# RWKV recurrence of a hybrid decoder layer: two full 32-bit products of each turn written as sums of products of high and low halves

## The chip, the cores and the metric

The kernel runs on one core of a Trainium2 chip. The core has five engines with a queue of instructions each: TensorE (PE in the profile; its weight loads are listed apart, as PEld), VectorE (DVE), ScalarE (ACT), GpSimd (POOL) and SyncE (SP), which here only issues DMAs. Every engine works through its own queue in order and waits for others at semaphores. The metric is the device time of one execution in microseconds (us); lower is better. The median of three runs of the kernel before is 944.3 us (944.24 to 944.64).

## The reference

One layer of a decoder for 512 tokens of width 1024, in float32. A combined projection feeds an RWKV-7 branch, a short convolution and a dilated attention; their gated sum and a SwiGLU follow. The change lies in the RWKV branch:

```python
xm = p + (token_shift(p) - p) * mu
r, k, v, wl, al, gl = jnp.split(xm, RWKV_SPLITS, axis=-1)
w_log = -jax.nn.softplus(-(w0 + jnp.tanh(wl) @ w_up)) - 0.5
a = jax.nn.sigmoid(a0 + al @ a_up)
g = jax.nn.sigmoid(gl) @ g_up                       # gate: 128 -> 512 channels
...
kk = heads(k * k_k)
kk = kk * lax.rsqrt(jnp.maximum(jnp.sum(kk * kk, axis=-1, keepdims=True), 1e-12))
k = k * (1 + (a - 1) * k_a)
...
_, y = lax.scan(rwkv7_step, state0, xs)             # the recurrence
...
return (y.reshape(bsz, seq, RWKV_WIDTH) * g.astype(jnp.float32)).astype(p.dtype)
```

The two products concerned are `sigmoid(gl) @ g_up` and the sum of `kk * kk` over the 64 channels of each head.

## The kernel before

All large products are already made of halves. A float32 operand x is split into a high part, x rounded to the type fp32r by a copy, and a low part, x less the high part, by a subtraction. A product then is three fp32r matmuls: high by high, low by high and high by low. For the weights ScalarE makes `w_hi` (L876), GpSimd makes `w_lo` in four instructions (L734), and SyncE loads `w_raw` two slots ahead.

The recurrence is worked through in four turns, T = 0 to 3, of 128 tokens each (`rwkv(T)`, one function on each of TensorE, VectorE and ScalarE). The small steps of a turn depend on each other across the engines. TensorE's gaps between them are filled with the rest of the big projection, `fill(count)` and `fill_steps(count)` at L2248: matmuls of 128 rows, 128 columns of weights and 512 tokens, three for each of `KT` = 8 slices, so 24 to a tile and 12 tiles (q = 0 to 11) to a turn. The tiles alternate between the PSUM banks 6 and 7. ScalarE copies each finished tile out (L964, L967, `copy_tile`), and tile q may only start when tile q - 2 has been copied (`spill_copied`). How many filler matmuls stand between two steps is written out by hand.

In this order TensorE does, in the first part of turn T: `fill(10)` and `loras(0)` (T = 0 only; the decay's and the in-context rate's up-projections, L2263), `fill(2)` or, for T > 0, `fill(6)`, then for T = 0 only `gate(0)` (L2269) and `turn_v(0)` (transposes of v, L2275), and in each turn the sum of squares (L2286), `fill(28)` or `fill(30)` and the transposes of the recurrence's operands. For T > 0 the calls `loras(T)`, `gate(T)`, `turn_v(T)` stand near the end of the turn before; the transposes of that turn's result y (`turn_y`, L2390) come ahead of them, except at the end of turn 0, where they come behind them and three filler matmuls later.

The other engines at these places: VectorE ends a turn with the chain that normalises y, whose last instruction multiplies by the gate (L1732, `y_ready`). Then it begins the next turn with `kk` (L1585), adds the biases to the up-projections (L1590, L1592), and waits for the sum of squares (L1597). ScalarE does tanh and sigmoid of the next turn's inputs (`lora_inputs`, L986, L987) near the end of a turn, then copies tiles; in the next turn it squares kk (L992), applies a sigmoid (L994), copies the gate out of PSUM (L997, L999), loads the table for the square root (L1002), takes it, and copies tile 0. All of these stand in one queue.

`need(signal)` waits for a signal of this turn. `Signal(name, per)` counts `per` increments a turn, and `at(turn, k)` is the value after the increment k of a turn.

Of the kernel before, what the change touches and what calls it, by code (L numbers as in the profile page):

```python
# [25 lines left out]
def hybrid_layer(nc, x, norm_mix_post, norm_ffn_pre, norm_ffn_post, w_in, rwkv_w_up, rwkv_a_up, rwkv_g_up,  # L26
# [77 lines left out]
    with ExitStack() as ctx:  # L104
# [26 lines left out]
        lora_up = fixed("lora_up", [P, RW])  # L131
        g_up = fixed("g_up", [P, RW])
# [80 lines left out]
        xs, _ = arena("xs", [P, NH, HD], e)  # L213
        k2, e = arena("k2", [P, NJ, P], o)
# [3 lines left out]
        assert o <= AT_YC, (o, AT_YC)  # L218
        rk, o = arena("rk", [P, NJ, P], AT_TAIL)
        state, o = arena("state", [P, NJ, 2, HD], o)  # L220
        g_tok, o = arena("g_tok", [P, NH, HD], o)
        y1, o = arena("y1", [P, NH, HD], o)
        y2, o = arena("y2", [P, NH, HD], o)
        ln_wb, o = arena("ln_wb", [P, 2, RW], o + 4 * NJ * P)
# [85 lines left out]
        params_loaded, ups_loaded = sem("params_loaded"), sem("ups_loaded")  # L310
# [28 lines left out]
        xm_ready, lora_ready, gate_ready = Signal("xm_ready"), Signal("lora_ready"), Signal("gate_ready")  # L339
        z_done, g_done = Signal("z_done"), Signal("g_done")  # L340
        z_ready, sig_ready, sums_run, exps_ready = Signal("z_ready"), Signal("sig_ready"), Signal("sums_run"), Signal("exps_ready")
        kk_ready, sq_ready, ssq_done, ssq_ready = Signal("kk_ready"), Signal("sq_ready"), Signal("ssq_done"), Signal("ssq_ready")
# [38 lines left out]
        form_hi_ready = after_turns(gate_ready)  # L381
        form_lo_made = after_turns(z_done)
        b_hi_made = after_turns(g_done)
        b_lo_made = after_turns(z_ready)
# [3 lines left out]
        t4_made = after_turns(kk_ready)  # L388
        t12_hi_made = after_turns(sq_ready)
# [175 lines left out]
        def _(sp):  # L565
# [25 lines left out]
            sp.dma_start(lora_up[0:HD, :], rwkv_w_up[0]).then_inc(ups_loaded, 16)  # L591
            sp.dma_start(lora_up[HD:P, :], rwkv_a_up[0]).then_inc(ups_loaded, 16)
            sp.dma_start(g_up[:], rwkv_g_up[0]).then_inc(ups_loaded, 16)
# [272 lines left out]
        def _(act):  # L866
# [70 lines left out]
            for n in range(5, N_RWKV + 2):  # L937
                high(n, raw_value(n), n % 2)
# [4 lines left out]
            def rwkv(T):  # L943
# [450 lines left out]
        def _(dve):  # L1394
# [178 lines left out]
            def rwkv(T):  # L1573
# [11 lines left out]
                v.tensor_tensor(kk[:], k_, par(C_KK), ALU.mult).then_inc(kk_ready.sem, 1)  # L1585
# [8 lines left out]
                last.then_inc(z_ready.sem, 1)  # L1594
                need(ssq_done)
                need(sq_ready)
# [514 lines left out]
        def _(pe):  # L2111
# [106 lines left out]
            pe.wait_ge(ups_loaded, 48)  # L2218

            def rwkv(T):  # L2220
# [64 lines left out]
                need(sq_ready)  # L2285
                t_.matmul(ps[:, 3], head_ones[:], sq[:].rearrange("p j t -> p (j t)"), start=True, stop=True).then_inc(ssq_done.sem, 1)  # L2286
# [524 lines left out]
```

## Time and profile before

| | before |
|---|---|
| median of 3 runs | 944.3 us (944.24 to 944.64) |
| profiled execution, its own time | 944.45 us |
| its span, first to last instruction | 942.4 us |
| TensorE busy | 934.0 us, 99% of the span |
| VectorE, ScalarE, GpSimd busy | 68%, 46%, 47% |
| mean granted clock of TensorE | 0.999 of full speed |
| TensorE busy from 83.7 to 405 us (most of the recurrence) | 321.27 of 321.3 us |

The busy time of TensorE is the union of its matmuls, which overlap: a matmul of 512 columns is listed with 0.39 us and followed by the next one after 0.23 us. So what a product costs is read from where the next one starts, not from its own duration. A timeline row names start, duration, engine, line, operation, output and inputs, and in brackets how long the engine had been idle and what ended that.

### The profile page before, as it was taken

What the parts mean: (1) busy time and instruction counts of PE and PEld (TensorE: products, weight loads), DVE (VectorE), ACT (ScalarE), POOL (GpSimd) and SP (SyncE); (2) the same over time, 40 slices, a digit from 0 to 9 for tenths busy, and PEclk for the clock granted to TensorE, in tenths of its full rate; (3) what the DMA queues carried; (4) which work ended last, traced back from release to release, by engine and by line L of the source; (5) the groups of instructions that cost most, each with busy time, mean ns of one, the idle gap of its engine ahead of it and who ended that gap; (6) DMA issues with size and microseconds to landing.
All of it is one profiled execution on the core that took longest, in us unless ns stands there. A gap on an engine that the chain in (4) does not pass through costs nothing.

```text
span 942.4 us, 16115 instructions
## 1 busy us (share of the span) xinstructions
PE 934.0 (99%) x6666; PEld 787.5 (84%) x6666; DVE 639.4 (68%) x814; ACT 432.0 (46%) x626; POOL 441.5 (47%) x325
## 2 busy tenths in 40 slices
PE   9999999999999999999999999999999999999997
PEld 7888877787887778777878888888999999988886
DVE  6877967766586756899675656988989898411114
ACT  6423515723461562337753425574556555322332
POOL 4884524334263245253145653514765565555551
PEclk9999999999999999999999999999999999999999
DMA  8323332342333265229144842286566656243312
GB/s 287 116 91 114 109 113 93 117 148 70 132 108 129 81 220 182 92 80 323 68 157 151 317 144 72 78 195 161 130 149 171 154 143 174 81 145 108 114 45 89
DMA packets 110805, 128.44 MB, mean 136 GB/s; under 512 B 3216, under 2 KB 87184, under 8 KB 110736
## 3 DMA queue, kind: packets, MB, share of 16 engines
q1 hardware_dynamic: 100224, 102.64, 33.9%
q0 software_dynamic: 2880, 10.49, 5.9%
q10 hardware_dynamic: 7632, 14.32, 4.0%
q8 instruction: 52, 0.85, 0.4%
q14 instruction: 17, 0.14, 0.0%
HBM read 100.70 MB, written 16.25 MB: 124 GB/s over the span
## 4 chain that ended last, share of the span: by engine, by line
PE 53%; issue 26%; POOL 16%; DVE 4%; ACT 1%; DMA 0%; POOLq 0%; DVEq 0%; ACTq 0%
POOL w_lo L734 15%; PE ps L2116 11%; PE ps L2117 11%; PE ps L2118 11%; PE ps L2654 5%; PE ps L2656 5%; PE ps L2655 5%; PE ps L2432 2%; PE ps L2467 1%; PE ps L2484 1%; DVE bias_dil L1504 1%; DVE x_ct L1513 1%; PE ps L2458 1%; PE ps L2161 0%; DVE rstd_x L1436 0%
## 5 line engine op out<-in xcount | busy, mean ns | idle before, releaser
L734 POOL TENSOR_TENSOR w_lo<-w_raw,w_hi 128x512 fp32r<-128x512 f32 x220 | 318.5, 1477 | 378.1 <-ACT w_hi L876 377.5
L876 ACT CAST w_hi<-w_raw 128x2048 fp32r<-128x2048 f32 x55 | 105.0, 1909 | 137.9 <-PE ps L2118 106.3
L2248 PE MATMUL ps<-a_hi,w_hi 128*128 128x512 f32 x384 | 154.7, 403 | 0.0
L2248 PE MATMUL ps<-a_lo,w_hi 128*128 128x512 f32 x384 | 152.0, 396 | 0.0
L2248 PE MATMUL ps<-a_hi,w_lo 128*128 128x512 f32 x384 | 151.0, 393 | 0.0
L2248 PEld LDWEIGHTS ps<-a_hi,w_hi 128*128 128x128 f32 x384 | 72.1, 188 | 17.1 <-issue 1.0
L2248 PEld LDWEIGHTS ps<-a_lo,w_hi 128*128 128x128 f32 x384 | 72.1, 188 | 15.5 <-issue 1.0
L2248 PEld LDWEIGHTS ps<-a_hi,w_lo 128*128 128x128 f32 x384 | 72.1, 188 | 15.1 <-ACT xs L1037 0.2
L2655 PE MATMUL ps<-form_lo,w_hi 128*128 128x256 f32 x256 | 72.4, 283 | 0.0
L2656 PE MATMUL ps<-form_hi,w_lo 128*128 128x256 f32 x256 | 72.4, 283 | 0.0
L2654 PE MATMUL ps<-form_hi,w_hi 128*128 128x256 f32 x256 | 72.4, 283 | 0.0
L2033 DVE TENSOR_TENSOR f_lo<-f_all,f_hi 128x1024 fp32r<-128x1024 f32 x11 | 16.1, 1467 | 82.8 <-ACT f_hi L1311 82.8
L2116 PE MATMUL ps<-w_hi,f_hi 128*128 128x512 f32 x176 | 68.5, 389 | 0.0
L2117 PE MATMUL ps<-w_lo,f_hi 128*128 128x512 f32 x176 | 68.5, 389 | 0.0
L2118 PE MATMUL ps<-w_hi,f_lo 128*128 128x512 f32 x176 | 68.5, 389 | 0.0
L821 POOL TENSOR_TENSOR w_lo<-w_raw,w_hi 128x1024 fp32r<-128x1024 f32 x16 | 41.0, 2561 | 28.0 <-ACT w_hi L1239 28.0
L967 ACT COPY spill_buf<-ps 128x512 f32<-128x512 f32 x36 | 20.9, 585 | 72.2 <-PE ps L2248 72.0
L2116 PE MATMUL ps<-a_hi,w_hi 128*128 128x512 f32 (+1 forms) x144 | 53.0, 368 | 0.0
L2117 PE MATMUL ps<-a_lo,w_hi 128*128 128x512 f32 (+1 forms) x144 | 52.6, 365 | 0.0
L2118 PE MATMUL ps<-a_hi,w_lo 128*128 128x512 f32 (+1 forms) x144 | 52.6, 365 | 0.0
L2655 PE MATMUL ps<-form_lo,late_hi 128*128 128x256 f32 x180 | 50.9, 283 | 0.0
L2656 PE MATMUL ps<-form_hi,late_lo 128*128 128x256 f32 x180 | 50.9, 283 | 0.0
(403 smaller groups left out, 2233.2 us busy)
## 6 DMA issues: line engine op xcount, KB each, us to landing
w_raw<-w_in SPq DMA_DIRECT2D x32, 1024.0 KB, 5.1
w_raw<-w_ffn_in SPq DMA_DIRECT2D x44, 512.0 KB, 4.7
spill<-spill_buf ACTq DMA_DIRECT2D x27, 512.0 KB, 3.1
w_raw<-w_ffn_out SPq DMA_DIRECT2D x11, 1024.0 KB, 5.0
late_lo<-w_raw POOLq DMA_DIRECT2D x14, 512.0 KB, 4.6
w_raw<-w_branch SPq DMA_DIRECT2D x5, 1024.0 KB, 9.0
g_ab<-spill SPq DMA_DIRECT2D x8, 512.0 KB, 4.8
w_raw<-w_out SPq DMA_DIRECT2D x4, 1024.0 KB, 7.5
```

The source lines that it names most:

```text
L734: g.tensor_tensor(w_lo[:, b, c], w_raw[:, b, c], w_hi[:, b, c].bitcast(F), ALU.subtract).then_inc(lo_ready, 1)
L821: g.tensor_tensor(w_lo[:, b, 0:2 * BLK], w_raw[:, b, 0:2 * BLK], w_hi[:, b, 0:2 * BLK].bitcast(F), ALU.subtract).then_inc(b_lo_made.sem, 1)
L876: s.copy(w_hi[:, b], w_raw[:, b]).then_inc(hi_ready, 1)
L967: s.copy(spill_buf[:, b, half], ps[:, 6 + half]).then_inc(spill_copied, 1)
L2116: t_.matmul(dst, w0, a0, start=first, stop=False)
L2117: t_.matmul(dst, w0, a1, start=False, stop=False)
L2118: return t_.matmul(dst, w1, a0, start=False, stop=last)
L2248: last = t_.matmul(ps[:, 6 + half], w[:, kt, half * P:(half + 1) * P], a, start=(kt == 0 and step == 0), stop=(kt == KT - 1 and step == 2))
L2432: last = t_.matmul(ps[:, LEFT_BANK[i]], w[:, kt, half * P:(half + 1) * P], a, start=(kt == 0 and step == 0), stop=(kt == KT - 1 and step = ...
L2654: t_.matmul(dst, hi[:, c], form_hi[f][:, k], start=first and k == 0, stop=False, skip_group_check=not first)
L2655: t_.matmul(dst, hi[:, c], form_lo[f][:, k], start=False, stop=False, skip_group_check=not first)
L2656: last = t_.matmul(dst, lo[:, c], form_hi[f][:, k], start=False, stop=k == KT // 2 - 1, skip_group_check=not first)
```

## The change

In each turn two products change form. `gate(T)` was one float32 matmul of `xm[:, RT-1]` (the sigmoid of the gate's inputs, 128 x 128) with `g_up` (128 x 512); now it is three fp32r matmuls, `gate_hi` with `g_up_hi`, `gate_hi` with `g_up_lo` and `gate_lo` with `g_up_hi`. The sum of squares was one float32 matmul of `head_ones` with `sq` (128 x 512); now it is two, with `sq_hi` and `sq_lo`, since the ones need no low part. The halves are made where the operand is at hand: ScalarE copies `gate_hi` behind the sigmoid, `sq_hi` behind the square, and `g_up_hi` once; VectorE subtracts `gate_lo` behind `kk`, `sq_lo` behind the additions for `sig`, and `g_up_lo` once, in place over `g_up`. The signals keep their semaphores and count two increments a turn.

```diff
@@ scalar engine, once, in the loop over the last slots before the recurrence
             for n in range(5, N_RWKV + 2):
+                if n == N_RWKV:
+                    act.wait_ge(ups_ready, 48)
+                    s.copy(g_up_hi[:], g_up[:]).then_inc(ups_ready, 1)
                 high(n, raw_value(n), n % 2)
@@ scalar engine, rwkv(T)
-                    s.activation(xm[:, RT - 1], xm[:, RT - 1], ACT.Sigmoid).then_inc(gate_ready.sem, 1)
+                    s.activation(xm[:, RT - 1], xm[:, RT - 1], ACT.Sigmoid).then_inc(gate_then_hi.sem, 1)
+                    act.wait_ge(gate_then_hi.sem, gate_then_hi.at(turn))
+                    s.copy(gate_hi[:], xm[:, RT - 1]).then_inc(gate_then_hi.sem, 1)
...
-                need(kk_ready)
-                s.activation(sq[:], kk[:], ACT.Square).then_inc(sq_ready.sem, 1)
-                need(z_ready)
+                need(kk_then_gate_lo)
+                s.activation(sq[:], kk[:], ACT.Square).then_inc(sq_then_hi.sem, 1)
+                need(sq_then_hi)
+                s.copy(sq_hi[:], sq[:].rearrange("p j t -> p (j t)")).then_inc(sq_then_hi.sem, 1)
+                need(z_then_sq_lo)
@@ vector engine, rwkv(T)
-                v.tensor_tensor(kk[:], k_, par(C_KK), ALU.mult).then_inc(kk_ready.sem, 1)
+                v.tensor_tensor(kk[:], k_, par(C_KK), ALU.mult).then_inc(kk_then_gate_lo.sem, 1)
+                if T == 0:
+                    dve.wait_ge(ups_ready, 49)
+                    v.tensor_tensor(g_up_lo[:], g_up[:], g_up_hi[:].bitcast(F), ALU.subtract).then_inc(ups_ready, 1)
+                need(gate_then_hi, 1)
+                v.tensor_tensor(gate_lo[:], xm[:, RT - 1], gate_hi[:].bitcast(F), ALU.subtract).then_inc(kk_then_gate_lo.sem, 1)
                 need(z_done)
...
-                last.then_inc(z_ready.sem, 1)
+                last.then_inc(z_then_sq_lo.sem, 1)
+                need(sq_then_hi, 1)
+                v.tensor_tensor(sq_lo[:], sq[:].rearrange("p j t -> p (j t)"), sq_hi[:].bitcast(F),
+                                ALU.subtract).then_inc(z_then_sq_lo.sem, 1)
                 need(ssq_done)
@@ tensor engine, gate(turn) and the sum of squares
-                    pe.wait_ge(gate_ready.sem, gate_ready.at(turn))
-                    t_.matmul(ps[:, 2], xm[:, RT - 1], g_up[:], start=True, stop=True).then_inc(g_done.sem, 1)
+                    pe.wait_ge(gate_then_hi.sem, gate_then_hi.at(turn, 1))
+                    pe.wait_ge(ups_ready, 49)
+                    t_.matmul(ps[:, 2], gate_hi[:], g_up_hi[:], start=True, stop=False)
+                    pe.wait_ge(ups_ready, 50)
+                    t_.matmul(ps[:, 2], gate_hi[:], g_up_lo[:], start=False, stop=False)
+                    pe.wait_ge(kk_then_gate_lo.sem, kk_then_gate_lo.at(turn, 1))
+                    t_.matmul(ps[:, 2], gate_lo[:], g_up_hi[:], start=False, stop=True).then_inc(g_done.sem, 1)
...
-                need(sq_ready)
-                t_.matmul(ps[:, 3], head_ones[:], sq[:].rearrange("p j t -> p (j t)"), start=True, stop=True).then_inc(ssq_done.sem, 1)
+                need(sq_then_hi, 1)
+                t_.matmul(ps[:, 3], head_ones[:].bitcast(R), sq_hi[:], start=True, stop=False)
+                need(z_then_sq_lo, 1)
+                t_.matmul(ps[:, 3], head_ones[:].bitcast(R), sq_lo[:], start=False, stop=True).then_inc(ssq_done.sem, 1)
```

TensorE's queue at the end of turn 0, where `gate(1)` stands, before; the rows are what it issues in order, and in brackets the semaphores that it waits for (`ident,xm` are the transposes of v, `ident,y_121` those of y):

```order
664 L2269 MATMUL ps<-g_up,xm 128x512 [waits gate_ready]
665 L2275 MATMUL ps<-ident,xm 128x128 [waits xm_ready]
666 L2275 MATMUL ps<-ident,xm 128x128 x3
667 L2248 MATMUL ps<-a_hi,w_hi 128x512
668 L2248 MATMUL ps<-a_lo,w_hi 128x512
669 L2248 MATMUL ps<-a_hi,w_lo 128x512
670 L2390 MATMUL ps<-ident,y_121 128x128 [waits y_ready]
```

The same place of the changed kernel:

```order
667 L2291 MATMUL ps<-g_up_hi,gate_hi 128x512 [waits ups_ready,gate_then_hi]
668 L2293 MATMUL ps<-g_up_lo,gate_hi 128x512 [waits ups_ready]
669 L2295 MATMUL ps<-g_up_hi,gate_lo 128x512 [waits kk_then_gate_lo]
670 L2301 MATMUL ps<-ident,xm 128x128 [waits xm_ready]
671 L2301 MATMUL ps<-ident,xm 128x128 x3
672 L2269 MATMUL ps<-a_hi,w_hi 128x512
...
675 L2418 MATMUL ps<-ident,y_125 128x128 [waits y_ready]
```

One matmul has become three, and the third waits for VectorE's second increment of `kk_then_gate_lo`, ahead of the place where TensorE waits for `y_ready`.

ScalarE's queue from the sigmoid at the end of turn 0 to the cast of the next weights in turn 1, before:

```order
92 L987 ACTIVATE xm<-xm 128x128
93 L967 COPY spill_buf<-ps 128x512 [waits spilled_odd,first_tile]
...
98 L992 ACTIVATE sq<-kk 128x512 [waits kk_ready]
99 L994 ACTIVATE sig<-sig 128x1024 [waits z_ready]
100 L997 COPY g_tok<-ps 128x256 [waits g_done]
101 L999 COPY g_tok<-ps 64x256 x2
102 L1002 ACT_TABLE_LOAD
103 L1002 ACTIVATE sq<-sq 128x512 [waits ssq_ready]
```

And in the changed kernel:

```order
95 L996 ACTIVATE xm<-xm 128x128
96 L998 CAST gate_hi<-xm 128x128 [waits gate_then_hi]
97 L976 COPY spill_buf<-ps 128x512 [waits spilled_odd,first_tile]
...
102 L1003 ACTIVATE sq<-kk 128x512 [waits kk_then_gate_lo]
103 L1005 CAST sq_hi<-sq 128x512 [waits sq_then_hi]
104 L1007 ACTIVATE sig<-sig 128x1024 [waits z_then_sq_lo]
105 L1010 COPY g_tok<-ps 128x256 [waits g_done]
106 L1012 COPY g_tok<-ps 64x256 x2
107 L1015 ACT_TABLE_LOAD
108 L1015 ACTIVATE sq<-sq 128x512 [waits ssq_ready]
```

The two new copies stand in front of the tile copy and in front of the sigmoid, and everything behind them on ScalarE moves back.

## Rows read from the trace of the kernel before

**Rows 1.** The page: busy time of TensorE, and its granted clock in 40 slices.

```profile
PE 934.0 (99%) x6666; PEld 787.5 (84%) x6666; DVE 639.4 (68%) x814; ACT 432.0 (46%) x626; POOL 441.5 (47%) x325
...
PEclk9999999999999999999999999999999999999999
```

**Rows 2.** Waits of TensorE: who it waited for, us in total, times, longest.

```profile
PE ps L2458 <- DVE p_buf L1767: 0.4, 1, 0.4
```

**Rows 3.** Timeline of TensorE, first part of turn 0.

```profile
92.57 1.02 PE L2269 MATMUL ps<-g_up,xm 128*128 128x512 f32 x2
...
93.43 0.60 PE L2275 MATMUL ps<-ident,xm 128*128 128x128 f32 x4
...
93.86 1.02 PE L2286 MATMUL ps<-sq,head_ones 128*128 128x512 f32 x2
...
94.96 0.39 PE L2248 MATMUL ps<-a_lo,w_hi 128*128 128x512 f32 x1
...
99.81 0.39 PE L2248 MATMUL ps<-a_lo,w_hi 128*128 128x512 f32 x1
...
113.64 0.39 PE L2248 MATMUL ps<-a_hi,w_lo 128*128 128x512 f32 x1
```

**Rows 4.** Timeline of ScalarE and of TensorE's weight loads, first part of turn 0.

```profile
92.58 1.06 ACT L994 ACTIVATE sig<-sig 128x1024 f32<-128x1024 f32 x1 [3.12 <-DVE sig L1592]
...
94.77 1.28 ACT L1002 ACT_TABLE_LOAD   x1
...
96.60 0.57 ACT L967 COPY spill_buf<-ps 128x512 f32<-128x512 f32 x1
...
97.29 0.19 PEld L2248 LDWEIGHTS ps<-a_hi,w_hi 128*128 128x128 f32 x1
```

**Rows 5.** Timeline of GpSimd and VectorE, turn 0; last row: groups of instructions by shape.

```profile
85.33 5.65 POOL L734 TENSOR_TENSOR w_lo<-w_raw,w_hi 128x512 fp32r<-128x512 f32 x4 [5.57 <-ACT w_hi L876]
...
87.04 1.57 DVE L1585 TENSOR_TENSOR kk<-xm,params 128x512 f32<-128x512 f32 x1
...
91.19 0.69 DVE L1590 TENSOR_TENSOR sig<-ps,params 128x512 f32<-128x512 f32 x1 [2.59 <-PE ps L2263]
...
L1471 DVE TENSOR_TENSOR xm<-proj 128x128 f32<-128x128 f32 x2 | 2.7, 1373 | 0.0
```

**Rows 6.** Timelines of ScalarE, TensorE and VectorE at the end of turn 0.

```profile
166.45 0.31 ACT L987 ACTIVATE xm<-xm 128x128 f32<-128x128 f32 x1
...
167.58 1.13 PE L2269 MATMUL ps<-g_up,xm 128*128 128x512 f32 x2
168.54 0.60 PE L2275 MATMUL ps<-ident,xm 128*128 128x128 f32 x4
...
168.47 0.69 DVE L1585 TENSOR_TENSOR kk<-xm,params 128x512 f32<-128x512 f32 x1
```

**Rows 7.** Groups by shape on VectorE; timeline of TensorE behind `loras(0)`.

```profile
L1675 DVE TENSOR_TENSOR tt<-tt,ps 128x128 f32<-128x128 f32 x16 | 4.6, 288 | 15.5 <-PE ps L2328 15.5
...
91.07 0.50 PE L2248 MATMUL ps<-a_hi,w_hi 128*128 128x512 f32 x1
...
91.41 0.39 PE L2248 MATMUL ps<-a_lo,w_hi 128*128 128x512 f32 x1
```

**Rows 8.** Timelines of ScalarE, weight loads, VectorE and TensorE at the end of turn 1.

```profile
245.48 0.57 ACT L964 COPY spill_buf<-ps 128x512 f32<-128x512 f32 x1
...
246.43 0.19 PEld L2248 LDWEIGHTS ps<-a_hi,w_hi 128*128 128x128 f32 x1
...
246.92 0.69 DVE L1585 TENSOR_TENSOR kk<-xm,params 128x512 f32<-128x512 f32 x1
...
248.73 1.12 PE L2269 MATMUL ps<-g_up,xm 128*128 128x512 f32 x2
```

**Rows 9.** Timelines of ScalarE and TensorE, first part of turn 2.

```profile
256.95 0.65 ACT L992 ACTIVATE sq<-kk 128x512 f32<-128x512 f32 x1
...
259.23 1.02 PE L2286 MATMUL ps<-sq,head_ones 128*128 128x512 f32 x2
```

More of the change, by code:

```diff
@@ L131, in hybrid_layer @@
         lora_up = fixed("lora_up", [P, RW])
+        g_up_lo = nc.alloc_sbuf_tensor_at("g_up_lo", [P, RW], R, offset=top[0])
         g_up = fixed("g_up", [P, RW])
@@ L213, in hybrid_layer @@
         xs, _ = arena("xs", [P, NH, HD], e)
+        gate_hi, e = arena("gate_hi", [P, P], o, R)
+        gate_lo, _ = arena("gate_lo", [P, P], e, R)
         k2, e = arena("k2", [P, NJ, P], o)
@@ L218, in hybrid_layer @@
         assert o <= AT_YC, (o, AT_YC)
+        sq_hi, _ = arena("sq_hi", [P, SEQ], AT_TAIL, R)
         rk, o = arena("rk", [P, NJ, P], AT_TAIL)
@@ L222, in hybrid_layer @@
         y1, o = arena("y1", [P, NH, HD], o)
+        sq_lo, _ = arena("sq_lo", [P, SEQ], o, R)
         y2, o = arena("y2", [P, NH, HD], o)
-        ln_wb, o = arena("ln_wb", [P, 2, RW], o + 4 * NJ * P)
+        g_up_hi, o = arena("g_up_hi", [P, RW], o, R)
+        ln_wb, o = arena("ln_wb", [P, 2, RW], o)
         y_a, _ = arena("y_a", [P, NJ, SEQ], (o + 512 + 511) // 512 * 512)
@@ L309, in hybrid_layer @@
         second_hi_ready, second_lo_ready = sem("second_hi_ready"), sem("second_lo_ready")
-        params_loaded, ups_loaded = sem("params_loaded"), sem("ups_loaded")
+        params_loaded, ups_ready = sem("params_loaded"), sem("ups_ready")
         piece_hi_ready, piece_lo_ready = sem("piece_hi_ready"), sem("piece_lo_ready")
@@ L338, in hybrid_layer @@
         y_c_ready = sem("y_c_ready")
-        xm_ready, lora_ready, gate_ready = Signal("xm_ready"), Signal("lora_ready"), Signal("gate_ready")
+        xm_ready, lora_ready, gate_then_hi = Signal("xm_ready"), Signal("lora_ready"), Signal("gate_then_hi", 2)
         z_done, g_done = Signal("z_done"), Signal("g_done")
-        z_ready, sig_ready, sums_run, exps_ready = Signal("z_ready"), Signal("sig_ready"), Signal("sums_run"), Signal("exps_ready")
-        kk_ready, sq_ready, ssq_done, ssq_ready = Signal("kk_ready"), Signal("sq_ready"), Signal("ssq_done"), Signal("ssq_ready")
+        z_then_sq_lo, sig_ready, sums_run, exps_ready = Signal("z_then_sq_lo", 2), Signal("sig_ready"), Signal("sums_run"), Signal("exps_ready")
+        kk_then_gate_lo, sq_then_hi, ssq_done, ssq_ready = Signal("kk_then_gate_lo", 2), Signal("sq_then_hi", 2), Signal("ssq_done"), Signal("ssq_ready")
         norm_ready, ops_ready, g_ready, rk_ready = Signal("norm_ready"), Signal("ops_ready"), Signal("g_ready"), Signal("rk_ready")
@@ L380, in hybrid_layer @@
         s_made = after_turns(lora_ready)
-        form_hi_ready = after_turns(gate_ready)
+        form_hi_ready = after_turns(gate_then_hi)
         form_lo_made = after_turns(z_done)
         b_hi_made = after_turns(g_done)
-        b_lo_made = after_turns(z_ready)
+        b_lo_made = after_turns(z_then_sq_lo)
         t1_made = after_turns(sig_ready)
@@ L387, in hybrid_layer @@
         t3_made = after_turns(exps_ready)
-        t4_made = after_turns(kk_ready)
-        t12_hi_made = after_turns(sq_ready)
+        t4_made = after_turns(kk_then_gate_lo)
+        t12_hi_made = after_turns(sq_then_hi)
         t12_lo_made = after_turns(ssq_done)
@@ L590, in _ @@
                 sp.dma_start(half8(1)[:, k0:k1], wi[1][:, k0:k1]).then_inc(second_loaded[i], 16)
-            sp.dma_start(lora_up[0:HD, :], rwkv_w_up[0]).then_inc(ups_loaded, 16)
-            sp.dma_start(lora_up[HD:P, :], rwkv_a_up[0]).then_inc(ups_loaded, 16)
-            sp.dma_start(g_up[:], rwkv_g_up[0]).then_inc(ups_loaded, 16)
+            sp.dma_start(lora_up[0:HD, :], rwkv_w_up[0]).then_inc(ups_ready, 16)
+            sp.dma_start(lora_up[HD:P, :], rwkv_a_up[0]).then_inc(ups_ready, 16)
+            sp.dma_start(g_up[:], rwkv_g_up[0]).then_inc(ups_ready, 16)
             sp.dma_start(ln_wb[:, 0], rwkv_ln_w.broadcast_to((P, RW))).then_inc(ln_loaded, 16)
@@ L2217, in _ @@
             pe.wait_ge(consts_ready, 1)
-            pe.wait_ge(ups_loaded, 48)
+            pe.wait_ge(ups_ready, 48)
             def rwkv(T):
```

2 lines of the change are left out of this document (1 added, 1 removed).

## The prediction

> **What bounds the kernel now.** I read the page first: TensorE is busy 934.0 of 942.4 us [rows 1], so nearly everything that it does lies on the path that sets the end, and the 8.4 us in which it is idle are mostly ahead of its first product and behind its last. The view of waits says the same: past the start TensorE is never idle for more than 0.4 us at once [rows 2]. Then I read the timelines at the places of the diff. Two kinds of thing count there: how much sooner TensorE is through a product, and whether something it waits for is there by then. No other engine's busy share matters, but the order in their queues does, since TensorE arrives at several waits with only tenths of a microsecond to spare.
>
> **What the products cost.** In turn 0 the gate's product starts at 92.57, the transposes behind it at 93.43: 0.86 us. The sum of squares starts at 93.86. The first filler behind it overlaps it, so I go by the second, at 94.96. The filler's pace is (113.64 - 99.81) / 61 = 0.227 us, 62 matmuls without a gap; so the first one counts from 94.73, and the sum of squares costs 0.87 us [rows 3]. The new ones have the shape of the filler, 128 x 128 weights and 512 columns, and I price them by its pace. Gate: 3 x 0.227 = 0.68, saves 0.18 a turn. Sum of squares: 2 x 0.227 = 0.45, saves 0.41 a turn. Four turns: 4 x 0.59 = 2.4 us. At the other gates the product takes 168.54 - 167.58 = 0.96 [rows 6]; the 0.1 more is paid by whatever comes first behind `loras` (91.07 to 91.41 is 0.34 for a filler too [rows 7]), so the saving is the same.
>
> By the Trainium skill ("FP8 and Floating Point Precision", TensorE Precision Notes) a true FP32 product takes four passes through the array, so that three and two passes would save a quarter and a half: with 0.86 us for four that is 0.22 and 0.43, and 2.6 us in four turns. The rows put a pass of the filler at 0.227 rather than 0.215, and I go by them.
>
> **Turn 0: the saving is lost again.** TensorE would reach tile 2 earlier by 0.59 us. Its first weight load is at 97.29. It waits for the copy of tile 0 on ScalarE, which starts at 96.60 and ends at 97.17 [rows 4]: 0.12 us between, so TensorE is already there just in time. That copy stands behind the square root, and that behind a table load from 94.77 to 96.05, which follows the gate's copies and the sigmoid at 92.58. The sigmoid is released by VectorE's additions (the bracket in its row), and these by `loras(0)`, which stands ahead of both changed products. So nothing in ScalarE's chain moves forward, and TensorE waits there for what it had saved: 0 instead of -0.59.
>
> The chain can move back. Between `kk`, which ends at 88.61, and the additions at 91.19 VectorE idles 2.59 us [rows 5]. Now `g_up_lo` and `gate_lo` stand there, while GpSimd subtracts until 90.98. `kk`, 128 x 512, took 1.57 us in that company, against 0.69 in the next turn [rows 6]. `g_up_lo` is of that size: until 90.2. For `gate_lo`, 128 x 128, the bounds are 0.29 us, the same shape without such company [rows 7], and 1.37 us, the same shape in the stretch before, where GpSimd was subtracting as well (L1471 in rows 5). That ends it between 90.5 and 91.6, and the additions are late by 0 to 0.4 us, and with them tile 0's copy and TensorE. I take 0.1: GpSimd stops at 90.98, so most of the upper bound can't be reached.
>
> The Trainium skill says of this ("SBUF — State Buffer", Who interferes with whom) that a VectorE instruction with two SBUF inputs contends with a GpSimd instruction that reads SBUF. The trace agrees, 1.57 against 0.69 us. By the same page (SBUF: two separate sides) the second one blocks until the first is done; so each of the two subtractions could wait for a whole GpSimd instruction, 5.65 / 4 = 1.4 us, which would end `gate_lo` at about 91.7 and cost 0.5 us here.
>
> **Turn 0 to 1: the third product of the gate waits.** Before, `gate(1)` needed only the sigmoid. Now its third matmul needs `gate_lo`, which VectorE makes behind `kk`, and `kk` stands behind the whole chain for y. It starts at 168.47 and ends at 169.16, whereas TensorE starts the gate at 167.58 [rows 6]. `gate_hi` is in time: sigmoid until 166.76, a copy of the same 0.31 us until about 167.1. The first two matmuls are through by 167.58 + 0.34 + 0.23 = 168.15. `gate_lo` takes 0.29 us [rows 7], until 169.45; with the 0.12 us seen between the copy and the weight load [rows 4] TensorE goes on at 169.57, and its first matmul after a break costs 0.34, until 169.91. Then come the transposes, which started at 168.54: +1.37 us. Bounds: without the 0.12 and with 0.23 for the matmul, +1.14; with a `gate_lo` as long as a 128 x 512 one (0.69), +1.8. Behind TensorE in this wait stand the transposes of v, three fillers, the transposes of y and with them ScalarE's next square; all of them move with it and have no one to wait for beyond it.
>
> **The other turns.** At the ends of turns 1 and 2 TensorE has waited for y already, ahead of `loras`. `kk` starts at 246.92, so `gate_lo` is there by about 247.9, and the third matmul is due at 248.73 + 0.57 = 249.3 [rows 8]: no wait, and 0.18 us saved at each of the two. In turns 1 to 3 the sum of squares is fed in time. In turn 2 ScalarE squares until 257.60, `sq_hi` (as long as the square, 0.65) is ready by 258.3, `sq_lo` (0.69) by 259.0; TensorE wants them at 259.23 and 259.46 [rows 9]. Turn 3 has the same spacing, turn 1 more room. So 0.41 us saved in each of three, and tile 0's copy is no limit there, since for T > 0 tile 2 comes much later than it.
>
> The new `gate_hi` delays ScalarE's copy of tile 9 at the ends of turns 1 and 2 by about 0.35 us, from 245.48 to 245.83, so that it ends at 246.40. Tile 11's first weights are loaded at 246.43 [rows 8]. With 0.12 us behind the copy that is 0.1 us late; with ScalarE's own wait for its sigmoid as another 0.1, 0.2. Part of it hides in the time between load and matmul. I take 0.05 for both turns together, with 0 and 0.4 as bounds.
>
> Costs of nothing: `g_up_hi` lies in one of ScalarE's idle stretches before the recurrence, `sq_lo` in VectorE's wait for the sum of squares, `sq_hi` of turn 0 in ScalarE's 3.12 us of idle time. Without that cover each costs its 0.6 to 0.7 us once or once a turn. In turns 1 to 3 `sq_hi` also pushes the table load, the root and the next cast of weights back by 0.5 us, while TensorE gets 0.4 earlier to what they feed.
>
> **The sum.** +0.1 (turn 0) + 1.37 (gate 1) - 2 x 0.18 (gates 2 and 3) - 3 x 0.41 (sums of squares) + 0.05 (tile 9) = -0.07 us. The profiled execution took 944.45 us; 944.4 then. Its span is 2.05 us less than its time, and it lies 0.15 above the median, so for the median: 944.2. With all low bounds (0, 1.14, 0) it is -0.45, 943.9; with all high ones (0.5, 1.8, 0.4) +1.1, 945.4.
>
> **Rivals.**
> 1. The whole saving arrives, 2.4 us, 941.9: `gate_lo` is never late, and tile 0's copy is early enough. For it: the products do get shorter, and TensorE is the bound. Against it: 168.47 for `kk` against 167.58 for the gate leaves no room, and the copy is 0.12 us ahead of its reader. 4 in 100.
> 2. ScalarE's delay costs more: the casts of the weights and GpSimd's low parts behind them arrive after TensorE in turns 1 to 3, or `sq_lo` misses its 0.4 us. Price: what exceeds the room, at most some 0.4 a turn, +1.2: 945.5. Against: for each of them I find room. 12 in 100.
> 3. Slower: TensorE's clock. A break of 1.4 us is longer than any it has in the recurrence now. If the granted clock falls from 2.4 to 1.2 GHz behind it, each filler takes another 0.227 us. From 9 of them on, 2 us, the result is slower by a measurable amount; with 16 it is +3.6, 947.8. For it: no break of that length is in the trace to show it harmless. Against: the 0.4 us wait is followed by full clock [rows 1, 2]. 6 in 100. The Trainium skill ("TensorE: Matmul & The Clock Gate", What's actually happening) has the gate follow how busy TensorE has been, with half speed as its resting state; by it one such break among full work would leave the clock as it is.
> 4. The change does not do what it says: an fp32r product on these operands is no faster than half of a float32 one, 0.43 us. Then the gates cost 1.29 instead of 0.86 and the sums nothing less: 4 x 0.43 + 1.37 = +3.1, 947.3. Against: the filler has the same form. 3 in 100.
>
> **How the numbers follow.** My forecast, 944.2, has 75 in 100, with 943.6 to 945.3 as its own range. Faster or slower counts from 0.2% on, 1.9 us, which is about what a measurement of this kernel tells from no change. Faster than 942.4: rival 1 and a rest, 0.06. Slower than 946.2: rivals 3 and 4, 0.09. No measurable difference: the forecast and rival 2, 0.85. The range reaches down to 943.0, between the low sum and rival 1, and up to 945.8, past rival 2; it leaves out rivals 1, 3 and 4.
>
> **What would show it.** Right: the third matmul of `gate(1)` with a wait for VectorE's `gate_lo` of about 1.4 us, the transposes behind it at +1.4; a wait for tile 0's copy at tile 2 of turn 0; 0.45 us from the sum of squares to the filler's pace; the gates of turns 2 and 3 without a wait; clock at full in all slices. Wrong: if tile 2 of turn 0 starts with TensorE still ahead by 0.5 us, if `gate_lo` at the end of turn 0 waits for something that I don't see, if TensorE waits for `sq_lo` or for GpSimd's low parts in turns 1 to 3, or if the clock drops.

## The result, and the profile after

| | before | after |
|---|---|---|
| median of 21 runs each | 944.41 us (944.15 to 945.81) | 945.88 us (945.05 to 946.45) |
| ratio, 95% interval | | 1.0013 [1.0007, 1.0019] |
| profiled execution, its own time | 944.45 us | 946.1 us |
| its span | 942.4 us | 944.0 us |
| mean granted clock of TensorE | 0.999 | 0.999 |

The changed kernel is 1.5 us slower (0.16% by the medians, 0.13% by the ratio). That is less than the 0.2% that the chances went by, but the interval of the ratio does not include 1, and the median lies 0.08 us above the upper end of my range. The sum of my steps had given -0.07 us.

The page of the changed kernel, first part and the clock, against [rows 1]: TensorE is busy for 1.2 us less, and the clock has not moved.

```profile
PE 932.8 (99%) x6670; PEld 789.1 (84%) x6670; DVE 649.1 (69%) x823; ACT 436.3 (46%) x635; POOL 442.0 (47%) x325
...
PEclk9999999999999999999999999999999999999999
```

The waits of TensorE (who it waited for, us in total, times, longest). Four are new, all within the recurrence, where TensorE had not waited before (the wait of [rows 2] is at 436.8 us, behind it):

```profile
PE ps L2295 <- DVE gate_lo L1603: 1.1, 1, 1.1
PE ps L2356 <- DVE wt L1686: 1.0, 1, 1.0
PE ps L2366 <- issue: 0.6, 1, 0.6
PE ps L2269 <- ACT spill_buf L976: 0.4, 1, 0.4
```

The first and the last I had forecast. The two in the middle I had not. To see what each is worth I took the start of the same product of the big projection in both traces, all through the recurrence, and looked where the difference (after less before, in us) changes:

| place | before | after | difference | this step | my term |
|---|---|---|---|---|---|
| ahead of the changed products | 79.69 | 79.79 | +0.10 | | |
| turn 0, two products shorter | 94.96 | 94.51 | -0.45 | -0.55 | -0.59 |
| turn 0, tile 2 | 97.50 | 97.62 | +0.12 | +0.57 | +0.69 |
| just ahead of gate 1 | 158.69 | 158.93 | +0.24 | +0.12 | 0 |
| behind gate 1 | 168.90 | 170.29 | +1.39 | +1.15 | +1.37 |
| sum of squares, turn 1 | 175.34 | 176.32 | +0.98 | -0.41 | -0.41 |
| behind gate 2 (and tile 9) | 250.04 | 250.82 | +0.78 | -0.20 | -0.16 |
| sum of squares, turn 2 | 260.32 | 260.71 | +0.39 | -0.39 | -0.41 |
| turn 2, behind the state product | 309.07 | 310.28 | +1.21 | **+0.82** | none |
| behind gate 3 (and tile 9) | 335.01 | 336.08 | +1.07 | -0.14 | -0.15 |
| sum of squares, turn 3 | 345.29 | 345.97 | +0.68 | -0.39 | -0.41 |
| turn 3, second level | 386.59 | 388.28 | +1.69 | **+1.01** | none |

The places that I priced, with the 0.12 that crept in ahead of gate 1, sum to -0.24 us. The two that I did not price come to 1.83 us.

**Turn 0**, TensorE of the changed kernel, against [rows 3]: gate 92.67 to 93.37, 0.70 us; sum of squares 93.72 to 94.28, 0.56 us, and the filler goes on. Then tile 2 waits for the copy of tile 0.

```profile
92.67 0.39 PE L2291 MATMUL ps<-g_up_hi,gate_hi 128*128 128x512 f32 x1
...
93.37 0.60 PE L2301 MATMUL ps<-ident,xm 128*128 128x128 f32 x4
93.72 0.48 PE L2312 MATMUL ps<-sq_hi,head_ones 128*128 128x512 f32 x1
94.04 0.40 PE L2314 MATMUL ps<-sq_lo,head_ones 128*128 128x512 f32 x1
94.28 0.39 PE L2269 MATMUL ps<-a_hi,w_hi 128*128 128x512 f32 x1
...
97.62 0.47 PE L2269 MATMUL ps<-a_hi,w_hi 128*128 128x512 f32 x1 [0.42 <-ACT spill_buf L976]
```

VectorE there, against [rows 5]: `g_up_lo` takes 1.78 and `gate_lo` 1.35 us beside GpSimd's subtractions (0.63 and 0.28 us alone, in rows below), and the additions start at 91.61 instead of 91.19, 0.32 us late beyond the 0.10 that the whole trace is late at that point.

```profile
88.63 1.78 DVE L1601 TENSOR_TENSOR g_up_lo<-g_up,g_up_hi 128x512 fp32r<-128x512 f32 x1
90.33 1.35 DVE L1603 TENSOR_TENSOR gate_lo<-xm,gate_hi 128x128 fp32r<-128x128 f32 x1
91.61 0.68 DVE L1608 TENSOR_TENSOR sig<-ps,params 128x512 f32<-128x512 f32 x1
```

**The gate of turn 1**, against [rows 6]: two products, 1.05 us of idle time, the third. VectorE makes `gate_lo` 0.61 us behind the start of `kk`.

```profile
168.65 0.69 DVE L1598 TENSOR_TENSOR kk<-xm,params 128x512 f32<-128x512 f32 x1
169.26 0.28 DVE L1603 TENSOR_TENSOR gate_lo<-xm,gate_hi 128x128 fp32r<-128x128 f32 x1
...
168.15 0.39 PE L2293 MATMUL ps<-g_up_lo,gate_hi 128*128 128x512 f32 x1
169.59 0.51 PE L2295 MATMUL ps<-g_up_hi,gate_lo 128*128 128x512 f32 x1 [1.05 <-DVE gate_lo L1603]
169.94 0.60 PE L2301 MATMUL ps<-ident,xm 128*128 128x128 f32 x4
```

**The hole in turn 2.** The state product is 32 products of 64 x 64. In the kernel before they are one block of 0.69 us, and the filler starts 0.63 us after the block's start:

```profile
307.82 0.69 PE L2349 MATMUL ps<-wt,qb 64*32 64x32 f32 x32
308.44 0.69 PE L2338 MATMUL ps<-state,ar 64*64 64x64 f32 x32
309.07 0.50 PE L2248 MATMUL ps<-a_hi,w_hi 128*128 128x512 f32 x1
```

In the changed kernel 31 of them run, then nothing for 0.59 us, then the last. "issue" says that nothing in the profile released it: no semaphore was late.

```profile
308.17 0.69 PE L2377 MATMUL ps<-wt,qb 64*32 64x32 f32 x32
308.80 0.69 PE L2366 MATMUL ps<-state,ar 64*64 64x64 f32 x31
310.08 0.27 PE L2366 MATMUL ps<-state,ar 64*64 64x64 f32 x1 [0.59 <-issue]
310.28 0.50 PE L2269 MATMUL ps<-a_hi,w_hi 128*128 128x512 f32 x1
```

**The wait in turn 3.** TensorE waits for a transpose (`wt`) on VectorE, which stands behind a masking operation (`qb`), and that behind an addition (`tt`). The three engines in the kernel before (the last row is one of the four subtractions by itself):

```profile
382.89 0.67 PE L2328 MATMUL ps<-qb,wt 64*64 64x32 f32 x32
...
383.70 0.89 DVE L1675 TENSOR_TENSOR tt<-tt,ps 128x128 f32<-128x128 f32 x3 [1.14 <-PE ps L2328]
384.62 0.48 DVE L1644 TENSOR_TENSOR qb<-tt,level_mask 128x256 f32<-128x256 f32 x1
...
382.29 5.20 POOL L734 TENSOR_TENSOR w_lo<-w_raw,w_hi 128x512 fp32r<-128x512 f32 x4 [11.24 <-ACT w_hi L876]
...
383.53 1.29 POOL L734 TENSOR_TENSOR w_lo<-w_raw,w_hi 128x512 fp32r<-128x512 f32 x1
```

And in the changed kernel:

```profile
383.55 0.67 PE L2356 MATMUL ps<-qb,wt 64*64 64x32 f32 x32
...
384.71 0.89 DVE L1696 TENSOR_TENSOR tt<-tt,ps 128x128 f32<-128x128 f32 x3 [1.49 <-PE ps L2356]
385.63 1.38 DVE L1665 TENSOR_TENSOR qb<-tt,level_mask 128x256 f32<-128x256 f32 x1
...
382.94 5.19 POOL L740 TENSOR_TENSOR w_lo<-w_raw,w_hi 128x512 fp32r<-128x512 f32 x4 [11.23 <-ACT w_hi L882]
...
385.43 1.30 POOL L740 TENSOR_TENSOR w_lo<-w_raw,w_hi 128x512 fp32r<-128x512 f32 x1
...
387.68 0.67 PE L2356 MATMUL ps<-qb,wt 64*64 64x32 f32 x32 [0.97 <-DVE wt L1686]
```

Taken one at a time, GpSimd's first three subtractions end at 383.57, 384.82 and 386.25 in the kernel before, and at 384.23, 385.47 and 386.73 in the changed one. In the kernel before `qb` starts while the second of them runs and ends at 385.10, 0.28 us behind it. In the changed kernel `qb` starts at 385.63, 0.16 us after the second has ended and with the third begun, and it ends at 387.01, 0.28 us behind the third. So `qb` costs 0.48 or 1.38 us by which side of 385.47 it starts on, and it would have started before that, had the addition ahead of it not come 0.35 us late: 1.16 us after the start of TensorE's product at 383.55, instead of 0.81 as before (product at 382.89).

### The profile page after: what moved, and what is told of

Its sections match the earlier page's. It is cut to its first block, busy times and chain, and to the rows that moved or that the text cites. A ratio compares the mean times of both kernels' runs of the same rounds, so it can differ in the third digit from the quotient of the medians.

```text
span 944.0 us, 16145 instructions
## 1 busy us (share of the span) xinstructions
PE 932.8 (99%) x6670; PEld 789.1 (84%) x6670; DVE 649.1 (69%) x823; ACT 436.3 (46%) x635; POOL 442.0 (47%) x325
## 4 chain that ended last, share of the span: by engine, by line
PE 51%; issue 26%; POOL 15%; DVE 3%; DMA 2%; ACT 1%; SPq 1%; POOLq 0%; DVEq 0%; ACTq 0%
POOL w_lo L740 15%; PE ps L2137 10%; PE ps L2138 10%; PE ps L2139 10%; PE ps L2682 5%; PE ps L2683 5%; PE ps L2684 5%; PE ps L2460 2%; DMA w_raw<-w_in 2%; PE ps L2495 1%; PE ps L2512 1%; DVE x_ct L1526 1%; PE ps L2486 1%; DVE bias_dil L1517 1%; PE ps L2182 0%
```

## The experiments

Each row has the median, the ratio to the kernel before on the same chip, and three readings at the places that I had not foreseen: TensorE's idle time ahead of the last of turn 2's state products ("hole"), how long after the start of TensorE's product turn 3's addition (`tt`) starts, and TensorE's wait for `wt`. All times are us. Each median is of 10 or 11 runs, those of pe_20 and pe_60 of 5 and 4. The first trace of the changed kernel has 0.59, 1.16 and 0.97 in the last three columns.

| run | median us | ratio, 95% interval | hole | `tt` after product | wait for `wt` |
|---|---|---|---|---|---|
| again | 945.70 | 1.0012 [1.0003, 1.0021] | 0.18 | 1.16 | 0.97 |
| gate_only | 945.90 | 1.0013 [1.0004, 1.0022] | 0.42 | 0.81 | none |
| ssq_only | 942.97 | 0.9984 [0.9975, 0.9993] | none | 0.80 | none |
| late_gate | 944.52 | 0.9999 [0.9990, 1.0008] | 0.35 | 1.15 | 0.98 |
| both_moves | 944.60 | 1.0000 [0.9991, 1.0009] | 0.35 | 1.16 | 0.98 |
| pe_20 | 949.00 | 1.0049 [1.0035, 1.0063] | none | 1.16 | 0.98 |
| pe_60 | 957.57 | 1.0139 [1.0124, 1.0155] | none | 1.16 | 0.97 |
| dve_7 | 943.17 | 0.9988 [0.9979, 0.9997] | 0.30 | 0.81 | none |
| after_dve7 | 944.71 | 0.9999 [0.9990, 1.0008] | 0.40 | 0.81 | none |
| after_shifted | 943.67 | 0.9989 [0.9980, 0.9998] | none | 0.80 | none |
| before_warm8 | 944.39 | 0.9997 [0.9988, 1.0006] | none | 0.81 | none |
| best | 942.23 | 0.9973 [0.9963, 0.9982] | none | 0.80 | none |

The kernel before had medians of 944.45, 944.35 and 944.56 us beside the first four, the second four and the last four.

**again**: the changed kernel, no edit.

> The changed kernel once more, for a second profile. In the first one 1.8 us were lost outside the products: TensorE had nothing to run for 0.6 us inside the state product of turn 2 (at 310.08, released by nothing that the profile shows), and in turn 3 a product waited 0.97 us for VectorE's transpose, whose masking operation before it took 1.38 instead of 0.42 us beside GpSimd's subtractions. Theory A: both belong to the changed kernel (where its instructions lie, and how the two engines' phases stand to each other), and both are there again, within 0.1 us of where they were. Theory B: both are chance of one execution, and one or both are missing or elsewhere; the profiled time is then 944.2 to 945.3 us. Median in either case 945.9 +- 0.2 us.

Theory A, as to the places: both losses are back at the same instructions. Only the hole's size varies (0.82 us lost in the first trace, 0.43 here).

**gate_only** and **ssq_only**: each takes the other half of the change out again, on all engines.

> Only the gate's up-projection in three products, the sum of squares in float32 as before. By the steps that I found: turn 0 +0.1 us (its VectorE additions come 0.3 us later, the gate itself is 0.16 us shorter), gate of turn 1 +1.17 us (its third product waits 1.05 us for gate_lo), gates of turns 2 and 3 -0.15 each: +1.0 us, 945.4 us, with neither of the two outer losses. If these losses hang on this half of the change alone (theory A, by where its instructions lie), 946.3 to 947.2. If the gate is not to blame for the slowdown (rival: the sum of squares is), 944.1.

> Only the sum of squares in two products, the gate in float32 as before. By the steps: -0.4 us in each of turns 1 to 3, and in turn 0 between 0 (the third tile still waits for ScalarE's copy, which comes after one more cast) and -0.4: -1.2 to -1.6 us, 942.8 to 943.2 us, and the verdict that the change's slowness comes from the gate. If the one more cast on ScalarE or the phase of the casts costs what the changed kernel lost in turn 3 (rival), one loss of 0.8 to 1.0 us is here too: 943.8 to 944.2.

The two halves have opposite signs. The sum of squares alone wins 1.5 us, and its trace shows -0.18 left of turn 0's saving (tile 2 still waits for the copy, but additions and copy are not late), then -0.32, -0.43, -0.42. The gate alone loses 1.5 us: +0.03 in turn 0, +1.25 at gate 1, +0.67 at the hole, -0.17 and -0.13 at gates 2 and 3. So the hole comes with the gate's half, and gate_only's time holds it: 945.90 lies between the 945.4 expected without the two losses and the 946.3 to 947.2 with them. The wait in turn 3 is in neither half alone.

**late_gate**: `gate(1)` moved behind the transposes of v and the three fillers.

```diff
                     loras(T + 1)
-                    gate(T + 1)
+                    if T > 0:
+                        gate(T + 1)
                     turn_v(T + 1)
                     fill_steps(rest - (40 if T == 0 else 44))
+                    if T == 0:
+                        gate(T + 1)
                     if T == 0:
                         turn_y()
```

> The changed kernel with the gate of turn 1 moved behind the turned values and the last three filler products of turn 0, where gate_lo is ready. If the wait for gate_lo is what that gate costs: the wait of 1.05 us of its third product is gone, turn 1 starts 1.1 us earlier and the median falls from 945.9 to 944.8 us. Rival: the time is only moved, since turn 0's end waits for something else (the turned outputs for VectorE's chain) or the gain shifts the phase of VectorE and GpSimd into another collision: 945.5 to 946 again. If it also removes the collision of turn 3: 943.8.

1.2 to 1.4 us faster than the changed kernel, as the first theory said (1.1 expected). VectorE's `gate_lo` comes at the same distance behind `kk`, but TensorE is busy until then:

```profile
168.83 0.40 PE L2293 MATMUL ps<-g_up_lo,gate_hi 128*128 128x512 f32 x1
169.21 0.50 PE L2295 MATMUL ps<-g_up_hi,gate_lo 128*128 128x512 f32 x1
169.56 0.60 PE L2418 MATMUL ps<-ident,y 128*128 128x128 f32 x4
```

**both_moves**: late_gate, and `g_up_lo` made in VectorE's idle time ahead of turn 0.

```diff
                     v.memset(state[:], 0.0).then_inc(state_zero, 1)
+                    dve.wait_ge(ups_ready, 49)
+                    v.tensor_tensor(g_up_lo[:], g_up[:], g_up_hi[:].bitcast(F), ALU.subtract).then_inc(ups_ready, 1)
...
-                if T == 0:
-                    dve.wait_ge(ups_ready, 49)
-                    v.tensor_tensor(g_up_lo[:], g_up[:], g_up_hi[:].bitcast(F), ALU.subtract).then_inc(ups_ready, 1)
```

> The changed kernel with two moves: the gate of turn 1 behind the turned values and the last filler products of turn 0 (as in late_gate), and g_up_lo made on VectorE in its idle time at 81.9 us, ahead of turn 0. Theory: turn 0's additions came 0.32 us late because g_up_lo (1.78 us beside GpSimd's subtractions) and gate_lo (1.35) stood ahead of them; with g_up_lo gone they start when loras is done, ScalarE's sigmoid, its copy of tile 0 and TensorE's third tile come 0.3 us earlier, and the median is 944.2 us (late_gate 944.52). The hole of some 0.5 us in turn 2's state product and the wait of 0.97 us in turn 3 are still there, since no engine has an instruction more or fewer at those places. Rival: g_up_lo was not what held them, 944.5.

The subtraction takes 0.63 us there instead of 1.78, and the additions wait for `loras` again, as in [rows 5]:

```profile
82.03 0.63 DVE L1549 TENSOR_TENSOR g_up_lo<-g_up,g_up_hi 128x512 fp32r<-128x512 f32 x1
...
89.57 0.60 DVE L1602 TENSOR_TENSOR gate_lo<-xm,gate_hi 128x128 fp32r<-128x128 f32 x1 [0.70 <-ACT gate_hi L998]
91.45 0.69 DVE L1607 TENSOR_TENSOR sig<-ps,params 128x512 f32<-128x512 f32 x1 [1.28 <-PE ps L2283]
```

From the first filler to tile 2 this kernel gains 0.27 us on the kernel before (+0.26 to -0.01), late_gate loses 0.03 (-0.27 to -0.24): 0.3 us, as expected. The medians (944.60 and 944.52) do not show it, and by themselves they would speak for the rival: the stretch ahead of the first filler varied by up to 0.8 us between traces.

**pe_20** and **pe_60**: both_moves, with the ten warm-up products in 2 or in 4 pieces (pe_20 is shown; pe_60 has `range(4)` and 32 columns).

```diff
-                t_.matmul(ps[:, 7, 0:P], all_ones[:], all_ones[:], start=True, stop=True)
+                for _ in range(2):
+                    t_.matmul(ps[:, 7, 0:64], all_ones[:], all_ones[:, 0:64], start=True, stop=True)
```

> both_moves, with each of the ten warm-up products at the kernel's start split into two of half the columns: the same columns, 20 TensorE instruction pairs more ahead of everything. Theory: the hole in turn 2's state product is TensorE's own instructions arriving late: a block of them is brought by the instruction queue in packets, and the gate's additional pair in turns 0, 1 and 2 moved the border of a block into the stretch where 64 small products follow each other in 1.3 us. A shift by 20 pairs moves the border: the hole leaves the last product of the state product, and it is either gone (-0.4 to -0.8 us against both_moves) or elsewhere among small products. The wait in turn 3, which is VectorE's, stays. Rival: the hole belongs to the place in the program (a semaphore, a bank) and stays at the 32nd product of turn 2's state product.

> The same with the warm-up products split into four: 60 TensorE instruction pairs more. Theory: as in pe_20, the hole is gone or elsewhere, and not where pe_20 has it. Rival: no change of place.

My edit was not free: a product of half the columns took as long as a whole one, so in pe_20 the first real product starts at 9.72 instead of 5.46 us, and in pe_60 at 18.25. That is nearly all of the difference to both_moves' median, and the times say nothing of the hole. The traces do: the state product is whole again, at the same place of the program, and from the first filler to the last pe_20 is 0.61 us shorter than both_moves, whose hole cost 0.57. So whether the hole is there depends on how many TensorE instructions stand ahead of it. It is not seen further up in these products either, although a break that belonged to one number in the stream would now lie 20 or 60 pairs earlier, still among the 64 small ones. pe_20:

```profile
312.58 0.69 PE L2366 MATMUL ps<-state,ar 64*64 64x64 f32 x32
313.20 0.50 PE L2269 MATMUL ps<-a_hi,w_hi 128*128 128x512 f32 x1
```

**dve_7**: both_moves, with seven more VectorE instructions ahead of turn 0.

```diff
-                    v.memset(state[:], 0.0).then_inc(state_zero, 1)
+                    for j in range(NJ):
+                        for c in range(2):
+                            last = v.memset(state[:, j, c], 0.0)
+                    last.then_inc(state_zero, 1)
```

> both_moves, with the clearing of the state on VectorE in eight pieces instead of one: 7 VectorE instructions more, in idle time ahead of turn 0. In turn 3 the addition of the second level (tt) started 1.16 us after TensorE's product in all three profiles with both halves of the change, and 0.81 us after it in those with one half or none; by that 0.35 us the masking operation behind it starts just after a new GpSimd subtraction has begun, instead of just before, and ends with that one, 1.3 us later. Theory: the 0.35 us are VectorE's instructions arriving late at one border of its stream, which nine additional VectorE instructions moved there. With 7 more the addition starts 0.81 us after the product again, the masking operation ends with the subtraction before, and 1.03 us are won: 943.2 us against both_moves' 944.2. Rival: the delay belongs to the phase of the engines, not to the stream: the wait of 0.97 us stays.

`tt` is on time and the wait is gone. That the median is just the 943.2 expected is in part luck, since both_moves had come out at 944.60 and not 944.2: from the first filler to the last dve_7 is 1.16 us shorter than both_moves, and the stretch ahead of it was shorter as well.

**after_dve7** and **after_shifted**: the changed kernel without the moves; the first with dve_7's edit, the second with that and

```diff
-    N_WARM = 10
+    N_WARM = 8
```

> The changed kernel as it is, with nothing but the clearing of the state in eight pieces on VectorE (7 VectorE instructions more ahead of turn 0). Theory (VectorE's stream is shifted, so that its addition in turn 3 isn't 0.35 us late and the masking operation doesn't wait out another GpSimd subtraction): the wait of 0.97 us in turn 3 is gone and the median is 1.0 us under the changed kernel's, 944.8 us. Rival (the moves, not the shift, made the difference in dve_7): 945.8.

> The changed kernel with the same seven VectorE instructions, and with 8 warm-up products on TensorE instead of 10 at the kernel's start, in the time in which it waits for the first inputs: 4 TensorE instruction pairs fewer ahead of everything, so that turn 2's state product stands 1 pair earlier in the stream than in the kernel before (in the changed kernel: 3 later). Theory: the hole of 0.3 to 0.8 us at the state product's 32nd product is gone too, and what is left is the sum of the steps that I predicted, with nothing beside them: 944.3 us, the kernel before's own time. Rival (the hole is gone only with many instructions more, as in pe_20 and pe_60): 944.8 as after_dve7. If fewer warm-ups cost anything, before_warm8 shows it.

**before_warm8**: the same line alone, in the kernel before.

> A control: the kernel before, with 8 warm-up products instead of 10 and nothing else. Theory: no change, 944.4 us. If fewer warm-ups slow the first products down (lower granted clock) or the shift by 4 pairs puts a hole elsewhere, 944.7 to 945.5, and the same is in after_shifted and best.

after_dve7 came as expected (944.71 for 944.8). Its VectorE in turn 3: the `tt` that was late is on time, and `qb` takes 0.48 us.

```profile
383.96 0.89 DVE L1699 TENSOR_TENSOR tt<-tt,ps 128x128 f32<-128x128 f32 x3 [1.14 <-PE ps L2359]
384.88 0.48 DVE L1668 TENSOR_TENSOR qb<-tt,level_mask 128x256 f32<-128x256 f32 x1
```

after_shifted has neither the hole nor the wait: four pairs fewer were enough, and the state product is whole.

```profile
308.31 0.69 PE L2369 MATMUL ps<-state,ar 64*64 64x64 f32 x32
308.93 0.50 PE L2272 MATMUL ps<-a_hi,w_hi 128*128 128x512 f32 x1
```

Its median, 943.67, is 0.6 under what I expected, and 0.9 under the kernel before beside it (944.56). By its trace the steps from the first filler to the last sum to -0.30 us. The rest lies outside them: the first filler starts 0.42 us earlier, and behind the recurrence another 0.29 us are gained, where TensorE idles less ahead of products that wait for a DMA and for `p_buf`. Both are of the size by which these stretches vary between traces, and why they came together here stays open. The control, before_warm8 (944.39), shows no cost of the fewer warm-ups.

**best**: dve_7 with `N_WARM = 8`.

> All four edits on the changed kernel: the gate of turn 1 later, g_up_lo early, the state cleared in eight pieces, 8 warm-up products. By the steps: dve_7 (943.17) less the hole of its trace (0.30 us idle, some 0.5 us in all): 942.7 us, some 1.7 us under the kernel before and at least level with ssq_only (942.97). If the hole stays, 943.2.

942.23 us, 2.3 us (0.27% by the ratio) under the kernel before and 0.5 under what I expected: the fastest of all, faster than the sum of squares alone. The difference to the kernel before goes from -0.43 at the start to -0.72 at tile 2, then to -0.97, -1.55 and -2.12 behind the sums of squares of turns 1, 2 and 3, with no loss between but 0.15 at gate 1. So 1.7 of the 2.3 us are steps within the recurrence. The trace of before_warm8 starts its fillers as early (-0.45) with a median only 0.17 us lower, so the 0.43 at the start is not counted as a gain of these edits.

## Why the prediction was wrong

**What held.** A product of this shape costs about the filler's pace: gate 0.70 us (I said 0.68), sum of squares 0.56 to the start of the first filler behind it (I said 0.45; its first product comes 0.32 us ahead of its second, and not 0.23). Together they bring TensorE 0.55 us forward in turn 0 (0.59), and the sum of squares saves 0.39 to 0.41 in each of turns 1 to 3 (0.41). Turn 0's saving is lost at tile 2, to the copy that I named; net +0.02 (I said +0.1). The third product of gate 1 waits for `gate_lo`, 1.05 us, and costs 1.15 (I said 1.37: VectorE starts `gate_lo` 0.61 us behind `kk`, where the row of `kk` lists 0.69, and TensorE goes on 0.05 us behind its end, where I had put 0.12). Gates 2 and 3 do not wait. The granted clock from 168.5 to 180 us, with the break of 1.05 us in it, is 1.00, so rival 3 is out; rival 4 is out by the 0.70; rival 1 by gate 1. Rival 2 is out as well, though its 945.5 is the nearest number: in turns 1 to 3 TensorE waits neither for `sq_lo` nor for GpSimd's low parts. My range reached up to 945.8 for the sake of that rival, so it is luck that the measured 945.88 lies so close to its end.

**What was short.** Additions late by 0.32 us in turn 0, where I took 0.1 because GpSimd would stop at 90.98. It did not: beside VectorE's subtractions its own four took 6.10 us instead of 5.65, until 91.54, and `gate_lo` ended 0.15 us behind them, at 91.69. The copy of tile 0 came 0.21 us late by that (96.91 for 96.60, less the 0.10), but it cost only 0.02, because the copy had 0.19 us of room where I had put none: TensorE starts the tile 0.14 us behind the copy's end (97.48 to 97.62), so in the kernel before it could have started at 97.31, and did at 97.50. ssq_only shows that room as its 0.18 us.

**The step that failed** is the one that I wrote behind gate 1: "all of them move with it and have no one to wait for beyond it", and with it the sum, which has terms for the changed places only and so puts every other place at nothing. It takes every later stretch as unchanged but for its start. The runs showed 1.83 us at two places that the diff does not touch, 0.82 in turn 2 and 1.01 in turn 3; the places with a term came to -0.24. Two things there depend on more than the start:

1. The number of TensorE instructions ahead. With one TensorE pair (a weight load and its matmul) more in each of turns 0 to 2 the 32nd state product of turn 2 came 0.2 to 0.6 us late, in all seven traces that have the gate's change and an unshifted TensorE stream; in none of the four that have that change and a stream shifted by -4 (twice), +20 or +60 pairs; nor in the kernel before, ssq_only or before_warm8. That it hangs on the place in the stream is shown, most plainly by after_dve7 and after_shifted, which differ in `N_WARM` alone. That it is the delivery of the instructions is only a reading: 64 products follow each other there in 1.3 us, no semaphore is late, and the trace shows a 16 KB packet of the instruction queue q8 at 307.6, 1.2 us ahead of the state product. But the kernel before and after_shifted, which have no hole, show such a packet 1.2 and 1.5 us ahead of theirs, and in pe_20 and pe_60 a border at the same place of the stream would have fallen among the same small products without leaving a hole. So the cause stays open. The Trainium skill ("Runtime: NRT & Kernel Launch", Instruction fetch mechanics) says that an engine's instructions are refilled in blocks of 16 KiB, 256 instructions, and that crossing a border costs little and is mostly hidden. The packet's size agrees; whether this break, which cost 0.43 to 0.82 us, is such a border no run here shows.
2. VectorE's place against GpSimd's subtractions. `tt` was late by 0.35 us in all six traces with nine VectorE instructions more ahead of it, and on time in the eight with 0, 4, 5 or 16 more (before and before_warm8, ssq_only, gate_only, and the four with the state cleared in pieces): its place in the stream again, shown. It is not GpSimd's phase: GpSimd's first subtraction ends 0.67 to 0.69 us behind the start of TensorE's product in the six late traces and in seven of the eight others. Why `tt` is late there stays open. Those 0.35 us became 1.01, because `qb` then starts behind the border of two GpSimd subtractions. In all fourteen traces this `qb` ends 0.28 us after a GpSimd subtraction does, and so does every other masking operation that GpSimd's subtractions lengthen, 70 in all. The Trainium skill ("SBUF — State Buffer", Summary: rules for kernel authors) has a VectorE instruction with two SBUF inputs blocked until the GpSimd instruction that came first is done, if that one reads SBUF. These rows agree, and so do those of turn 0: `kk`, `g_up_lo` and `gate_lo` end 0.54, 0.55 and 0.15 us behind a GpSimd subtraction, each somewhat less than it takes alone (0.69, 0.63 and 0.28), as `qb` does with 0.28 against 0.42. I had taken the rule only as an upper bound for turn 0, with 91.7 for the end of `gate_lo`; it was 91.69.

With both shifted away (after_shifted) the changed kernel is not slower than the one before: its steps within the recurrence sum to -0.30 us, where my sum had -0.07.

## What to carry to other kernels

When everything waits for one engine with tenths to spare, a change that adds instructions is not over where it ends: compare the start of the same instruction in both traces from the first change to the last, and a step in the difference at an untouched line is a finding of its own. A loss of under 1 us at such a place can be moved by a few harmless instructions in idle time ahead of it; test it so before blaming the change. And judge the parts alone: here the sum of squares won 1.5 us and the gate lost 1.5: 1.25 at one product that had been put ahead of its operand and 0.67 at a place that the change does not touch, less 0.3 saved at the later gates.

## What the runs showed of the hardware

- The VectorE operations with two SBUF inputs that ran beside a series of GpSimd subtractions were not slowed by a share: each ended behind the end of one of the subtractions, by a time that was the same for the same shape. A 128 x 256 masking operation took 0.42 us alone, and 0.48, 0.76 or 1.38 us by where in GpSimd's 1.30 us it started, and ended 0.28 us behind it every time. GpSimd is held up in turn: the subtraction during which the masking operation ran on took 1.45 to 1.48 us instead of 1.27 to 1.30.
- A break of 0.2 to 0.6 us in TensorE's work without any semaphore behind it, near the end of 64 small products, that stays at one place of the program from run to run, varies in length, and is gone when the stream ahead is 4 pairs shorter or 20 or 60 longer. Its cause is open.
- Float32 warm-up products of 128, 64 and 32 columns at the kernel's start, two pairs of weight load and matmul each, took the same time each: from 1.17 us, 20 pairs until 5.46, 40 until 9.72, 80 until 18.25, which is 0.21 us a pair.
